# A layer kernel whose streamed operands lose the four padding columns between prompt and sample, and whose product halves meet at a bank border

## The chip, the core and the metric

The kernel runs on one core of a Trainium2 chip. A core has TensorE (PE: matmuls and their weight loads), VectorE (DVE), ScalarE (ACT), GpSimd (POOL) and SyncE (SP), which here issues loads; on-chip memory (SBUF) with 128 partitions, and PSUM, eight banks of 512 fp32 columns a partition, into which TensorE writes. The metric is the device time of one execution in microseconds.

## The reference

One layer of a streaming encoder, for 512 prompt frames of one new stream and 32 sample frames of a running one, width 1024:

```python
xn = rms_norm(x, g_mix_norm)
z = xn @ w_in
c_q, c_kv, k_r, u, gate_a, gate_b = jnp.split(z, IN_SPLITS, axis=-1)
...
attn = chunk_causal_mla(q_nope, q_rope, k_nope, kr_all, v, q_pos, jnp.arange(n_k))
u_c, lru_buf_new = causal_dwconv(u, lru_buf, lru_conv_w, lru_conv_b)
rec, h_last = rg_lru(u_c, h0, w_rg, b_rg, w_ig, b_ig, lru_lambda)
mixed = jax.nn.sigmoid(gate_a) * attn + jax.nn.sigmoid(gate_b) * rec
x = x + mixed @ w_out
up = rms_norm(x, g_ffn_norm) @ w_up
up_c, ffn_buf_new = causal_dwconv(up, ffn_buf, ffn_conv_w, ffn_conv_b)
gate, val = jnp.split(up_c, 2, axis=-1)
x = x + (jax.nn.silu(gate) * val) @ w_down
```

The convolutions have width 4 (u) and 3 (up), and start from stored rows of the sample's stream, or from zeros for the prompt; the recurrence starts from a stored state for the sample and from zero for the prompt.

## The kernel before

Channels lie on the 128 partitions and frames along a row. All frames are handled together: columns 0 to 511 are the prompt, then come four padding columns (`PAD`), then the 32 sample columns, so a row has `T` = 548 columns and a half `HT` = 274. The padding is there for the convolutions and the recurrence, which run once over the whole row: the last padding columns take the stored rows of the sample (L735 for U, L1555 for the up-projection), and the column before the sample restarts the recurrence (L587, L589).

The large products (`product`, L1612; `gate_half`, L1758; `output_product`, L1841; `last_product`, L2045) are fp32 products in three parts: the weight is split in a high part `w_hi` (ScalarE, L668) and a low part `w_lo` (VectorE, L1101), the operand likewise (`xnh`/`xnl`, `mxh`/`mxl`, `x2h`/`x2l`, `hh`/`hl`, type fp32r), and high x high, high x low and low x high are added up in PSUM. An item is 128 output channels: for each of 8 blocks k of 128 input channels (22 in the down-projection) three parts, and for each part two matmuls, one per half of the row, in two neighbouring banks. So an item of 8 blocks is 48 matmuls of 274 columns, each with its own weight load.

The order of the work:

1. Load and transpose x, its splits, and the products for the latents (L1651), which are 416 columns wide.
2. Twelve items of the first products (`FIRST`): gates A0, B0, U0 to U7, A1, B1, two bank pairs in turn (`pair`). VectorE evacuates each with `evacuate_first` (L1434) times the inverse norms `rsT`; for a U item the convolution (L1202, L1203, VectorE), the recurrence gates (`lru`, L1680, fp32 with the convolved `uc` as operand), activations on ScalarE (L745, L748, L755, L764, L771, L797) and the recurrence (L1214) follow. GpSimd keeps the tail of each U row (`conv_tail`, L582).
3. Eight head pairs of attention (`attend`), between which twelve more gate items are computed half by half (`gate_half`), and in which VectorE multiplies recurrence and gate (`gated_recurrence`, L1343) and ScalarE and VectorE evacuate keys, queries and values (L819, L850, L1283).
4. Eight items of the output product, the second norm, then 44 items of the up-projection (a loop of four with four bank pairs, `up_pair`). VectorE evacuates each (L1549), splits the weights two items ahead, sets two stored columns (L1555) and convolves (L1560 to L1565); for every second gate and value row ScalarE takes the SiLU (L1056) and GpSimd multiplies, rounds and subtracts (L630, L632, L634) to `hh` and `hl`. VectorE waits for these before it reuses the rows (L1561).
5. Eight items of the down-projection, 132 matmuls each; evacuation with the residual (L1585, L1582), transposes and stores.

Matmul j of a pair writes columns 0 to 273 of bank `2 * rank + j`, and an evacuation reads two runs of 274:

```python
PS[:, 2 * rank + j, 0:HT]
return PS[:, 2 * (g % 2):2 * (g % 2) + 2, 0:HT]
tt(halves(u_r[:, LEAD:]), up_pair(r), halves(rsT[:, :]), ALU.mult).then_inc(s_free, 1)
```

Of the kernel before, what the change touches and what calls it, by code (L numbers as in the profile page):

```python
# [15 lines left out]
F32 = mybir.dt.float32  # L16
# [4 lines left out]
P = 128  # L21
# [112 lines left out]
def layer(nc, i, c, o):  # L134
# [3 lines left out]
    with ctx:  # L138
# [33 lines left out]
        U = fixed("U", [P, KD, LEAD + T])  # L172
# [6 lines left out]
        QT = fixed("QT", [P, 4, T])  # L179
        xs = place  # L180
# [26 lines left out]
        TB = -(-T * 4 // 32) * 32  # L207
# [5 lines left out]
        ucs = [at(f"uc{s}", [P, T], uc_at[s]) for s in range(6)]  # L213
        a2 = at("a2", [P, 4, T], qt_at)
        ths = [a2[:, 3, :] if th_at[s] is None else at(f"th{s}", [P, T], th_at[s]) for s in range(6)]
        lruw = at("lruw", [P, 4, 2, P], v_at)
        tmps = [at("tmp0", [P, T], v_at + 4 * 2 * P * 4), at("tmp1", [P, T], p_at + 3 * TB)]

        assert region + D * 4 + 4 * P * 4 + NTT * P * 4 <= region + KD * (LEAD + T) * 4
# [22 lines left out]
        upx = fixed("upx", [P, 4, LEAD + T])  # L242
        uct = fixed("uct", [P, 4, T])
# [255 lines left out]
        def _(pool):  # L499
# [157 lines left out]
        def _(act):  # L657
# [71 lines left out]
            def first_tap(g, n):  # L729
# [5 lines left out]
                link(nc.scalar.activation(u_n[:, LEAD + S0 - 3:LEAD + S0], vec[:, V_CS:V_CS + 24].rearrange("p (j m) -> p m j", j=3)[:, n, :],  # L735
# [1390 lines left out]
```

## Time and profile before

| | |
|---|---|
| runs, us | 875.20, 871.04, 874.24 |
| median, us | 874.24 |
| span of the profiled execution, us | 872.8 |
| PE busy | 852.5 us, 98% |
| DVE busy | 568.6 us, 65% |
| ACT busy | 365.7 us, 42% |
| POOL busy | 192.9 us, 22% |
| clock granted to TensorE, mean | 0.992 |
| HBM traffic over the span | 72 GB/s |

The span goes from the first to the last instruction of the profiled execution; no separate time of that execution is listed, and the span lies among the three runs' times. PE is the matmuls, PEld their weight loads, which lie beside them. The page also follows the chain that ended last back from the end, gives groups of instructions by line and shape with the idle time before them and what ended it, and the trace can be asked for the instructions in order of time. Matmul records overlap, so a mean duration is not the time that one takes in a stream. The chain's shares by engine are PE 88%, ACT 6%, DVE 3%, issue 2%.

### The profile page before, as it was taken

What the parts mean: (1) busy time and instruction counts of PE and PEld (TensorE: products, weight loads), DVE (VectorE), ACT (ScalarE), POOL (GpSimd) and SP (SyncE); (2) the same over time, 40 slices, a digit from 0 to 9 for tenths busy, and PEclk for the clock granted to TensorE, in tenths of its full rate; (3) what the DMA queues carried; (4) which work ended last, traced back from release to release, by engine and by line L of the source; (5) the groups of instructions that cost most, each with busy time, mean ns of one, the idle gap of its engine ahead of it and who ended that gap; (6) DMA issues with size and microseconds to landing.
All of it is one profiled execution on the core that took longest, in us unless ns stands there. A gap on an engine that the chain in (4) does not pass through costs nothing.

```text
span 872.8 us, 16689 instructions
## 1 busy us (share of the span) xinstructions
PE 852.5 (98%) x6522; PEld 817.2 (94%) x6522; DVE 568.6 (65%) x998; ACT 365.7 (42%) x608; POOL 192.9 (22%) x206
## 2 busy tenths in 40 slices
PE   5999999899999999999999999999999999999998
PEld 5999898789999899877999999999999999999998
DVE  5586678867675676887656888778777876222121
ACT  5534959655655466556245221222212221122121
POOL 4021123202021121121140333323333234010000
PEclk8999999899999999999999999999999999999999
DMA  8433311131120101100223233232322323233321
GB/s 245 116 90 95 89 49 38 40 80 38 28 54 24 53 25 29 50 1 26 73 75 95 75 94 96 72 96 74 94 81 87 94 68 93 82 105 99 104 56 39
DMA packets 114466, 63.73 MB, mean 73 GB/s; under 512 B 7660, under 2 KB 112878, under 8 KB 114412
## 3 DMA queue, kind: packets, MB, share of 16 engines
q1 hardware_dynamic: 112428, 59.25, 24.0%
q0 software_dynamic: 1936, 3.70, 1.7%
q8 instruction: 38, 0.62, 0.3%
q14 instruction: 16, 0.13, 0.1%
q10 hardware_dynamic: 48, 0.02, 0.0%
HBM read 59.85 MB, written 2.70 MB: 72 GB/s over the span
## 4 chain that ended last, share of the span: by engine, by line
PE 88%; ACT 6%; DVE 3%; issue 2%; DMA 0%; POOL 0%; SPq 0%; ACTq 0%; DVEq 0%; POOLq 0%
PE PS L1612 49%; PE PS L1758 9%; PE PS L1841 6%; PE PS L1775 4%; PE PS L1813 4%; PE PS L1651 3%; PE PS L1717 2%; PE PS L1795 2%; PE PS L2045 2%; PE PS L1713 2%; PE PS L1749 2%; PE PS L1739 1%; PE PS L1680 1%; PE PS L1624 1%; PE PS L1820 1%
## 5 line engine op out<-in xcount | busy, mean ns | idle before, releaser
L668 ACT ACTIVATE w_hi<-w_raw 128x1024 fp32r<-128x1024 f32 (+2 forms) x102 | 105.5, 1035 | 316.5 <-PE PS L1612 301.4
L1101 DVE TENSOR_TENSOR w_lo<-w_raw,w_hi 128x1024 fp32r<-128x1024 f32 (+2 forms) x102 | 124.8, 1224 | 114.5 <-ACT w_hi L668 114.3
L1612 PE MATMUL PS<-x2h,w_hi 128*128 128x274 f32 x704 | 147.6, 291 | 0.0
L1612 PE MATMUL PS<-x2h,w_lo 128*128 128x274 f32 x704 | 147.0, 290 | 0.0
L1612 PE MATMUL PS<-x2l,w_hi 128*128 128x274 f32 x704 | 146.9, 290 | 0.0
L1612 PEld LDWEIGHTS PS<-x2l,w_hi 128*128 128x128 f32 x704 | 112.0, 189 | 0.0
L1612 PEld LDWEIGHTS PS<-x2h,w_hi 128*128 128x128 f32 x704 | 111.9, 189 | 0.1
L1612 PEld LDWEIGHTS PS<-x2h,w_lo 128*128 128x128 f32 x704 | 111.4, 189 | 0.0
L630 POOL TENSOR_TENSOR uct<-uct 128x548 f32<-128x548 f32 x22 | 30.2, 1373 | 176.4 <-DVE uct L1565 176.4
L1612 PE MATMUL PS<-hh,w_hi 128*128 128x274 f32 x308 | 64.7, 291 | 0.0
L1612 PE MATMUL PS<-hh,w_lo 128*128 128x274 f32 x308 | 64.6, 291 | 0.0
L1612 PE MATMUL PS<-hl,w_hi 128*128 128x274 f32 x308 | 64.2, 290 | 0.0
L1758 PE MATMUL PS<-xnh,w_hi 128*128 128x274 f32 x192 | 57.6, 300 | 0.2 <-DVE KT L1283 0.2
L1758 PE MATMUL PS<-xnl,w_hi 128*128 128x274 f32 x192 | 55.6, 290 | 0.0
L1758 PE MATMUL PS<-xnh,w_lo 128*128 128x274 f32 x192 | 55.6, 289 | 0.0
L887 ACT ACTIVATE PT<-PS 128x128 f32<-128x128 f32 (+4 forms) x72 | 31.3, 435 | 53.1 <-PE PS L1795 49.3
L1775 PE MATMUL PS<-KT,QT 100*128 100x128 f32 (+3 forms) x128 | 47.8, 456 | 3.5 <-ACT Pn L873 1.7
L562 POOL TENSOR_TENSOR rot<-Qn,rope 128x320 f32<-128x320 f32 x16 | 14.9, 948 | 162.7 <-DVE Qn L1273 162.7
L1612 PEld LDWEIGHTS PS<-hh,w_hi 128*128 128x128 f32 x308 | 48.9, 189 | 0.1
L1612 PEld LDWEIGHTS PS<-hl,w_hi 128*128 128x128 f32 x308 | 48.9, 190 | 0.0
L1612 PEld LDWEIGHTS PS<-hh,w_lo 128*128 128x128 f32 x308 | 48.8, 189 | 0.0
L1813 PE MATMUL PS<-PT,V 128*128 128x128 f32 x320 | 47.0, 278 | 0.0
(291 smaller groups left out, 1851.2 us busy)
## 6 DMA issues: line engine op xcount, KB each, us to landing
w_raw<-in_w_up_dram SPq DMA_DIRECT2D x44, 512.0 KB, 3.9
w_raw<-in_w_in_dram SPq DMA_DIRECT2D x24, 512.0 KB, 3.9
w_raw<-in_w_down_dram SPq DMA_DIRECT2D x16, 512.0 KB, 4.3
w_raw<-in_w_out_dram SPq DMA_DIRECT2D x8, 512.0 KB, 4.3
w_raw<-in_w_down_dram SPq DMA_DIRECT2D x8, 384.0 KB, 4.0
xnat<-in_x_prompt_dram SPq DMA_DIRECT2D x4, 512.0 KB, 5.4
w_raw<-in_w_in_dram SPq DMA_DIRECT2D x4, 416.0 KB, 7.4
wq<-in_w_q_b_dram SPq DMA_DIRECT2D x8, 192.0 KB, 2.5
```

The lines of the kernel that those rows point to most:

```text
L630: nc.gpsimd.tensor_tensor(uct[:, 2 + j, :], uct[:, j, :], uct[:, 2 + j, :], ALU.mult).then_inc(s_h2, 1)
L668: nc.scalar.activation(hi[:, slot % 2, 0:n], raw[:, slot % 4, 0:n], ACT.Copy).then_inc(s_hi, 1)
L887: nc.scalar.activation(PT[:, b, 0:w], PS[:, 6 + b, 0:w], ACT.Copy).then_inc(s_ptf, 1)
L1101: tt(lo[:, slot % 2, 0:n], raw[:, slot % 4, 0:n], hi[:, slot % 2, 0:n].bitcast(F32), ALU.subtract).then_inc(s_lo, 1)
L1612: last = mm(PS[:, 2 * rank + j, 0:HT], w[:, slot % 2, cols], x[:, k0 + k, j * HT:(j + 1) * HT], start=(k0 + k == 0 and first), stop=(k0 + ...
L1651: last = mm(PS[:, 3 + t, 0:LAT], x[:, k, w0:w0 + P], w[:, t4 % 2, cols], start=(k == 0 and w is hi and x is xnh), stop=(k == KD - 1 and w ...
L1713: last = mm(bank[:, a * P:(a + 1) * P], latT[:, k0:k0 + P], wkv[:, q % 2, 0, :], start=True, stop=True)
L1717: last = mm(bank[:, a * 2 * QK:(a + 1) * 2 * QK], cqT[:, k, c0 - p0:c0 - p0 + P], wq[:, q % 2, k, :], start=(k == 0), stop=(k == NQ - 1))
L1758: last = mm(PS[:, j, 0:HT], w[:, item % 2, cols], x[:, k, j * HT:(j + 1) * HT], start=(k == 0 and first), stop=(k == KD - 1 and w is lo))
L1775: mm(bank[:, 0:w], QT[0:QK + NT, 2 * par + h, t * P:(t + 1) * P], KT[0:QK + NT, 2 * par + h, 0:w], start=True, stop=True).then_inc(s_s, 1)
L1813: last = mm(values_bank(h)[:, t * P:(t + 1) * P], V[:, par, a, h:h + 2, :].rearrange("p h n -> p (h n)"), PT[:, b, a * P:(a + 1) * P], sta ...
L1841: last = mm(PS[:, 2 * (r % 4) + j, 0:HT], w[:, cols], x[:, k, j * HT:(j + 1) * HT], start=(k == 0 and first), stop=(k == KD - 1 and w is w ...
```

## The change

`T` becomes 544 and `HT` 272: xT, rsT, the split operands (`xnh`, `mxh`, `x2h`, `hh` and their low parts), the gates, the query columns and the sums have the sample right behind the prompt. The buffers on which a convolution or the recurrence runs (U, uc, th, a2, tmp, upx, uct) keep the padding: they have `TU` = 548 columns, and the fp32 products on `uc` halves of `HU` = 274. Where data go from one form to the other, the operation is split in a prompt part (512 columns) and a sample part (32): the evacuation of U and of the up-projection (`evacuate_padded`, 8 and 44 times), the product of recurrence and gate (8 times, written back without padding), and GpSimd's product of SiLU and value (22 times). Gate items and the others are evacuated in one operation.

In PSUM, the first half of a `product` is written to the last 272 columns of its bank and the second to the first 272 of the next one (`joined_half`), so that both are one run of 544 columns (`joined`), which an evacuation reads as such. `gate_half`, `output_product` and `last_product` write to the start of their banks as before.

The memsets of the padding of xT, cqT, rsT and sums go; two for U and upx come. All matmuls stay, 4704 of them with 272 columns in place of 274. As the rows are shorter, buffers move: the starts of w_hi, w_lo and of all split operands in SBUF were odd multiples of 32 bytes (but hl) and are multiples of 64 now.

```diff
-PAD = 4
-S0 = SEQ + PAD
+S0 = SEQ
 T = S0 + DEC
 HT = T // 2
+PAD = 4
 LEAD = 4
+US = SEQ + PAD
+TU = US + DEC
+HU = TU // 2
...
-        U = fixed("U", [P, KD, LEAD + T])
+        U = fixed("U", [P, KD, LEAD + TU])
...
+        place = max(place, qt_at + 4 * TU * 4)
...
-        upx = fixed("upx", [P, 4, LEAD + T])
-        uct = fixed("uct", [P, 4, T])
+        upx = fixed("upx", [P, 4, LEAD + TU])
+        uct = fixed("uct", [P, 4, TU])
...
+        def joined(bank):
+
+            return PS[:, bank:bank + 2, :].rearrange("p a b -> p (a b)")[:, 512 - HT:512 + HT]
+
+        def joined_half(bank, j):
+
+            return PS[:, bank + j, 0:HT] if j else PS[:, bank, 512 - HT:512]
+
         def pair(g):
 
-            return PS[:, 2 * (g % 2):2 * (g % 2) + 2, 0:HT]
+            return joined(2 * (g % 2))
...
-                    nc.gpsimd.tensor_tensor(uct[:, 2 + j, :], uct[:, j, :], uct[:, 2 + j, :], ALU.mult).then_inc(s_h2, 1)
+                    h_j = uct[:, 2 + j, 0:T]
+                    nc.gpsimd.tensor_tensor(h_j[:, 0:SEQ], uct[:, j, 0:SEQ], h_j[:, 0:SEQ], ALU.mult)
+                    nc.gpsimd.tensor_tensor(h_j[:, S0:], uct[:, j, US:], uct[:, 2 + j, US:], ALU.mult).then_inc(s_h2, 1)
                     pool.wait_ge(s_h2, it * 2 + (j + 1))
-                    nc.gpsimd.tensor_copy(one(hh, it * 2 + j, slice(None))[:, 0], uct[:, 2 + j, :]).then_inc(s_hh, 1)
+                    nc.gpsimd.tensor_copy(one(hh, it * 2 + j, slice(None))[:, 0], h_j).then_inc(s_hh, 1)
                     pool.wait_ge(s_hh, it * 2 + (j + 1))
-                    nc.gpsimd.tensor_tensor(one(hl, it * 2 + j, slice(None))[:, 0], uct[:, 2 + j, :],
+                    nc.gpsimd.tensor_tensor(one(hl, it * 2 + j, slice(None))[:, 0], h_j,
                                             one(hh, it * 2 + j, slice(None))[:, 0].bitcast(F32), ALU.subtract).then_inc(s_hl, 1)
...
-                nc.scalar.activation(uc(n), u_n[:, 1:1 + T], ACT.Identity, scale=vec[:, V_CW + n:V_CW + n + 1],
+                nc.scalar.activation(uc(n), u_n[:, 1:1 + TU], ACT.Identity, scale=vec[:, V_CW + n:V_CW + n + 1],
...
-            nc.vector.memset(xT[:, :, SEQ:S0], 0.0)
-            nc.vector.memset(cqT[:, :, SEQ:S0], 0.0)
             nc.vector.memset(ones[:, :], 1.0)
             nc.vector.memset(zero[:, :], 0.0)
-            nc.vector.memset(rsT[:, SEQ:S0], 1.0)
-            nc.vector.memset(sums[:, SEQ:S0], 1.0)
...
+            nc.vector.memset(U[:, :, LEAD + SEQ:LEAD + US], 0.0)
...
-                h_p = U[:, p, LEAD:]
+                h_p, g_p = U[:, p, LEAD:], gate("B", p)
                 dve.wait_ge(s_ends, 1)
                 dve.wait_ge(s_gt, gate_count("B", p))
-                stt(h_p, gate("B", p), 1.0, h_p, ALU.add, ALU.mult).then_inc(s_hb, 1)
+                stt(h_p[:, 0:SEQ], g_p[:, 0:SEQ], 1.0, h_p[:, 0:SEQ], ALU.add, ALU.mult)
+                stt(h_p[:, S0:T], g_p[:, S0:], 1.0, h_p[:, US:], ALU.add, ALU.mult).then_inc(s_hb, 1)
...
+            def evacuate_padded(dst, bank):
+
+                tt(dst[:, 0:SEQ], joined(bank)[:, 0:SEQ], rsT[:, 0:SEQ], ALU.mult)
+                tt(dst[:, US:TU], joined(bank)[:, S0:], rsT[:, S0:], ALU.mult).then_inc(s_free, 1)
+
             def evacuate_first(g):
 
                 kind, n = FIRST[g]
                 dve.wait_ge(s_used, I_IN + g + 1)
-                dst = U[:, n, LEAD:] if kind == "U" else gate(kind, n)
-                tt(halves(dst), pair(g), halves(rsT[:, :]), ALU.mult).then_inc(s_free, 1)
+                if kind == "U":
+                    evacuate_padded(U[:, n, LEAD:], 2 * (g % 2))
+                else:
+                    tt(gate(kind, n), pair(g), rsT[:, :], ALU.mult).then_inc(s_free, 1)
...
+            nc.vector.memset(upx[:, :, LEAD + SEQ:LEAD + US], 0.0)
...
-                    tt(halves(u_r[:, LEAD:]), up_pair(r), halves(rsT[:, :]), ALU.mult).then_inc(s_free, 1)
+                    evacuate_padded(u_r[:, LEAD:], 2 * r)
...
-                tt(halves(yT[:, m % 2, :]), pair(m), halves(xT[:, m, :]), ALU.add).then_inc(s_free, 1)
+                tt(yT[:, m % 2, :], pair(m), xT[:, m, :], ALU.add).then_inc(s_free, 1)
...
-                                last = mm(PS[:, 2 * rank + j, 0:HT], w[:, slot % 2, cols], x[:, k0 + k, j * HT:(j + 1) * HT],
+                                last = mm(joined_half(2 * rank, j), w[:, slot % 2, cols], x[:, k0 + k, j * HT:(j + 1) * HT],
...
-                        last = mm(PS[:, 4 + 2 * a + j, 0:HT], lruw[:, n % 4, a, :], uc(n)[:, j * HT:(j + 1) * HT], start=True, stop=True)
+                        last = mm(PS[:, 4 + 2 * a + j, 0:HU], lruw[:, n % 4, a, :], uc(n)[:, j * HU:(j + 1) * HU], start=True, stop=True)
```

VectorE's program in the up-projection, one item (the third) (st_127 is the buffer of kept tails). Before:

```order
L1549 TENSOR_TENSOR upx<-PS,rsT 128x548
L1101 TENSOR_TENSOR w_lo<-w_raw,w_hi 128x1024
L1555 COPY upx<-vec 128x2
L1561 TENSOR_SCALAR uct<-upx,vec 128x548
L1562 SCALAR_TENSOR_TENSOR uct<-upx,vec,uct 128x548
L1564 COPY st_127<-upx 128x4
L1565 SCALAR_TENSOR_TENSOR uct<-upx,vec,uct 128x548
```

And with the change, where L1443 and L1444 are `evacuate_padded`:

```order
L1443 TENSOR_TENSOR upx<-PS,rsT 128x512
L1444 TENSOR_TENSOR upx<-PS,rsT 128x32
L1115 TENSOR_TENSOR w_lo<-w_raw,w_hi 128x1024
L1575 COPY upx<-vec 128x2
L1581 TENSOR_SCALAR uct<-upx,vec 128x548
L1582 SCALAR_TENSOR_TENSOR uct<-upx,vec,uct 128x548
L1584 COPY st_127<-upx 128x4
L1585 SCALAR_TENSOR_TENSOR uct<-upx,vec,uct 128x548
```

The evacuation has become two instructions, and the second carries the signal that the banks are free; the rest is in the order it had. On TensorE no instruction changes its place.

## Rows read from the trace of the kernel before

**Rows 1.** The page: busy time, share of the span and instructions, all engines.

```profile
PE 852.5 (98%) x6522; PEld 817.2 (94%) x6522; DVE 568.6 (65%) x998; ACT 365.7 (42%) x608; POOL 192.9 (22%) x206
```

**Rows 2.** The chain that ended last, share of the span by line.

```profile
by line: PE PS L1612 49.4%; PE PS L1758 8.5%; PE PS L1841 5.7%; PE PS L1775 3.7%; PE PS L1813 3.5%; PE PS L1651 2.9%; PE PS L1717 2.0%; issue 2.0%; PE PS L1795 2.0%; PE PS L2045 1.9%; PE PS L1713 1.6%; PE PS L1749 1.6%; PE PS L1739 0.8%; PE
```

**Rows 3.** The same chain in order of time: start us, us, what.

```profile
85.93 0.74 DVE U L1434
...
114.70 0.74 DVE U L1434
...
228.56 1.11 PE PS L1749 x10
...
746.75 16.87 PE PS L1612 x132
```

**Rows 4.** TensorE by line and shape: xcount | busy us, mean ns | idle before.

```profile
L1612 PE MATMUL PS<-x2h,w_hi 128*128 128x274 f32 x704 | 147.6, 291 | 0.0
...
L1612 PE MATMUL PS<-hh,w_hi 128*128 128x274 f32 x308 | 64.7, 291 | 0.0
...
L1758 PE MATMUL PS<-xnh,w_hi 128*128 128x274 f32 x192 | 57.6, 300 | 0.2 <-DVE KT L1283 0.2
...
L1612 PE MATMUL PS<-xnh,w_hi 128*128 128x274 f32 x192 | 42.3, 302 | 0.0
...
L1841 PE MATMUL PS<-mxh,w_hi 128*128 128x274 f32 x96 | 20.7, 297 | 0.5 <-DVE mxl L1357 0.5
...
L2045 PE MATMUL PS<-hh,w_hi 128*128 128x274 f32 x44 | 10.3, 294 | 0.0
...
L1841 PE MATMUL PS<-mxh,out_hi 128*128 128x274 f32 x32 | 6.7, 291 | 0.0
```

**Rows 5.** TensorE in order of time, latent products: start us, us, engine, line.

```profile
25.16 0.35 PE L1651 MATMUL PS<-w_hi,xnh 128*128 128x416 f32 x1
...
32.71 0.35 PE L1651 MATMUL PS<-w_hi,xnl 128*128 128x416 f32 x1
```

**Rows 6.** VectorE in order of time, around 37 us and in the up-projection.

```profile
36.59 0.69 DVE L1153 COPY rsT<-PS 128x512 f32<-128x512 f32 x1 [4.12 <-PE PS L1663]
37.20 0.18 DVE L1154 COPY rsT<-PS 128x32 f32<-128x32 f32 x1
37.30 1.22 DVE L1101 TENSOR_TENSOR w_lo<-w_raw,w_hi 128x1024 fp32r<-128x1024 f32 x1
...
509.90 0.72 DVE L1549 TENSOR_TENSOR upx<-PS,rsT 128x548 f32<-128x548 f32 x1
```

**Rows 7.** Stretches: us, then busy us (xcount) of PE, PEld, DVE, ACT, POOL; granted clock.

```profile
170.00:377.00 207.00, 206.54 (x1639) 185.95 (x1640) 147.13 (x321) 114.71 (x232) 34.47 (x38) 1.00 0.15 40
...
377.00:386.00 9.00, 8.77 (x72) 7.00 (x70) 8.79 (x14) 5.86 (x12) 3.31 (x5) 1.00 0.01 2
...
464.00:746.00 282.00, 282.00 (x2207) 281.83 (x2205) 217.53 (x314) 68.63 (x74) 93.66 (x70) 1.00 0.29 85
...
153.80:160.60 6.80, 6.00 (x22) 4.70 (x21) 5.12 (x7) 4.73 (x10) 0.00 (x0) 0.50 0.36 93
```

**Rows 8.** GpSimd by line and shape.

```profile
L630 POOL TENSOR_TENSOR uct<-uct 128x548 f32<-128x548 f32 x22 | 30.2, 1373 | 176.4 <-DVE uct L1565 176.4
...
L529 POOL TENSOR_TENSOR krot<-nat,rope_in 128x80 f32<-128x80 f32 x4 | 1.3, 353 | 34.0 <-DVE nat L1194 34.0
```

**Rows 9.** TensorE in order of time, pairs of the first products.

```profile
60.10 0.41 PE L1612 MATMUL PS<-xnl,w_hi 128*128 128x274 f32 x2
60.35 0.42 PE L1612 MATMUL PS<-xnh,w_lo 128*128 128x274 f32 x2
60.62 0.41 PE L1612 MATMUL PS<-xnh,w_hi 128*128 128x274 f32 x2
```

**Rows 10.** Weight loads by line and shape.

```profile
L1612 PEld LDWEIGHTS PS<-x2h,w_hi 128*128 128x128 f32 x704 | 111.9, 189 | 0.1
...
L1749 PEld LDWEIGHTS PS<-wkv,latT 128*128 128x128 f32 x144 | 17.4, 191 | 1.9 <-ACT QT L921 1.2 <-ACT Qn L823 0.7
```

More of the change, by code:

```diff
@@ L204, in layer @@
         att_end = place
-        TB = -(-T * 4 // 32) * 32
+        TB = -(-TU * 4 // 32) * 32
         v1_at = v_at + NKT * 3 * VD * 4
@@ L212, in layer @@
         assert v1_at + 3 * TB <= p_at and p_at + 4 * TB <= att_end - NTT * 2 * HR * 4 and v_at + 4 * 2 * P * 4 + TB <= v1_at
-        ucs = [at(f"uc{s}", [P, T], uc_at[s]) for s in range(6)]
-        a2 = at("a2", [P, 4, T], qt_at)
-        ths = [a2[:, 3, :] if th_at[s] is None else at(f"th{s}", [P, T], th_at[s]) for s in range(6)]
+        ucs = [at(f"uc{s}", [P, TU], uc_at[s]) for s in range(6)]
+        a2 = at("a2", [P, 4, TU], qt_at)
+        ths = [a2[:, 3, :] if th_at[s] is None else at(f"th{s}", [P, TU], th_at[s]) for s in range(6)]
         lruw = at("lruw", [P, 4, 2, P], v_at)
-        tmps = [at("tmp0", [P, T], v_at + 4 * 2 * P * 4), at("tmp1", [P, T], p_at + 3 * TB)]
-        assert region + D * 4 + 4 * P * 4 + NTT * P * 4 <= region + KD * (LEAD + T) * 4
+        tmps = [at("tmp0", [P, TU], v_at + 4 * 2 * P * 4), at("tmp1", [P, TU], p_at + 3 * TB)]
+        assert region + D * 4 + 4 * P * 4 + NTT * P * 4 <= region + KD * (LEAD + TU) * 4
         xnat = at("xnat", [P, NTT, D], zone)
@@ L567, in mix @@
             def mix(p):
-                o_p, h_p = gate("A", p), U[:, p, LEAD:]
+                o_p, h_p = gate("A", p), U[:, p, LEAD:LEAD + T]
                 pool.wait_ge(s_o, 3 * p + 3)
@@ L580, in conv_tail @@
                 pool.wait_ge(s_free, n + 3)
-                tail = U[:, n, LEAD + T - 72:].rearrange("p (a b) -> p a b", b=36)[:, :, 33:36]
+                tail = U[:, n, LEAD + TU - 72:].rearrange("p (a b) -> p a b", b=36)[:, :, 33:36]
                 nc.gpsimd.tensor_copy(st[:, 2:8, n].rearrange("p (a b) -> p a b", a=2), tail).then_inc(s_tail, 1)
@@ L744, in lru_gates @@
                 act.wait_ge(s_tail, n + 1)
-                step.on(nc.scalar.activation(halves(u_n), PS[:, 4:6, 0:HT], ACT.Sigmoid, bias=vec[:, V_BR + n:V_BR + n + 1]))
+                step.on(nc.scalar.activation(halves(u_n), PS[:, 4:6, 0:HU], ACT.Sigmoid, bias=vec[:, V_BR + n:V_BR + n + 1]))
                 if n >= 2:
                     act.wait_ge(s_iu, n - 1)
-                nc.scalar.activation(halves(tmps[n % 2][:, :]), PS[:, 6:8, 0:HT], ACT.Sigmoid,
+                nc.scalar.activation(halves(tmps[n % 2][:, :]), PS[:, 6:8, 0:HU], ACT.Sigmoid,
                                      bias=vec[:, V_BI + n:V_BI + n + 1]).then_inc(s_lrui, 1)
@@ L789, in last_states @@
                 blocks = slice(0, KD)
-                ends = U[:, blocks, LEAD + T - 72:].rearrange("p n (a b) -> p n a b", b=36)[:, :, :, 35]
+                ends = U[:, blocks, LEAD + TU - 72:].rearrange("p n (a b) -> p n a b", b=36)[:, :, :, 35]
                 nc.scalar.activation(st[:, 0:2, blocks].rearrange("p a n -> p n a"), ends, ACT.Copy).then_inc(s_ends, 1)
@@ L1511, in _ @@
             dve.wait_ge(s_ri, NP_)
-            o_p, h_p = gate("A", 7), U[:, 7, LEAD:]
+            o_p, h_p = gate("A", 7), U[:, 7, LEAD:LEAD + T]
             dve.wait_ge(s_o, 3 * NP_)
@@ L1559, in up_block @@
                         dve.wait_ge(s_hl, it * 2 + 2)
-                    link(ts(dst, u_r[:, 2:2 + T], w[0], bias if is_value else None, ALU.mult, ALU.add) if is_value
-                         else ts(dst, u_r[:, 2:2 + T], w[0], None, ALU.mult))
-                    link(stt(dst, u_r[:, 3:3 + T], w[1], dst, ALU.mult, ALU.add))
-                    tail = u_r[:, LEAD + T - 72:].rearrange("p (a b) -> p a b", b=36)[:, :, 34:36]
+                    link(ts(dst, u_r[:, 2:2 + TU], w[0], bias if is_value else None, ALU.mult, ALU.add) if is_value
+                         else ts(dst, u_r[:, 2:2 + TU], w[0], None, ALU.mult))
+                    link(stt(dst, u_r[:, 3:3 + TU], w[1], dst, ALU.mult, ALU.add))
+                    tail = u_r[:, LEAD + TU - 72:].rearrange("p (a b) -> p a b", b=36)[:, :, 34:36]
                     step.on(nc.vector.tensor_copy(out_[:, bass.ds(it * 2 + (2 * b + m0), 1)][:, 0], tail))
-                    stt(dst, u_r[:, 4:4 + T], w[2], dst, ALU.mult, ALU.add).then_inc(s_gc, 1)
+                    stt(dst, u_r[:, 4:4 + TU], w[2], dst, ALU.mult, ALU.add).then_inc(s_gc, 1)
             up_block(0, 0)
```

16 lines of the change are left out of this document (8 added, 8 removed).

## Prediction

> **What bounds the kernel now.** I read the page's busy shares first. TensorE is busy for 852.5 of 872.8 us [rows 1], so an operation on another engine costs time only where it makes TensorE stop, and a column taken from a matmul is worth time only where TensorE itself is the chain. That is told by the chain that ended last, summed by line [rows 2]. The 274-column products make up L1612 49.4%, L1758 8.5%, L1841 5.7% and L2045 1.9% of the span, together 65.5% of 872.8 = 572 us. In order of time the same chain leaves TensorE in a few places only, among them from 85.93 us (the evacuation of U on VectorE, then ScalarE until 104.9) and from 114.70 us [rows 3]. The reader is to see that both begin with the very line that the change splits in two (L1434). Late in the program nothing leaves TensorE: 132 matmuls take 16.87 us as one piece [rows 3].
>
> How many matmuls there are: 704 + 308 + 192 + 192 + 96 + 32 + 44 = 1568 for the first of three operand pairs, and as many for each of the other two, so 4704 [rows 4]. What one costs can't be read from "mean 290 ns", since the records overlap; it is the distance from start to start. In a stream without a stop that is 16.87 us / 132 = 127.8 ns [rows 3]. So 572 us are about 4,470 matmuls on the chain; the other 230 stand beside ScalarE and VectorE work, and a column less in them is worth nothing.
>
> **The change, part by part.**
>
> *Two columns fewer in each of 4704 matmuls (274 to 272).* The trace has no 272, so the price of a column comes from two sizes of the same kind of product. The 416-column matmuls start at 25.16 and, 40 later, at 32.71 us: 188.8 ns each [rows 5]. The slope is (188.8 - 127.8)/(416 - 274) = 0.43 ns a column, and two are 0.86 ns. If the time were strictly in proportion, two columns would be 127.8 x 2/274 = 0.93 ns. I take 0.90, the middle. On the chain: 4,470 x 0.90 = 4.0 us gained. From below the price is bounded by nothing at all (rival B), from above by 1.7 ns (rival A).
>
> [...]
>
> *Evacuations of U and of the up-projection in two pieces* (8 and 44 times, L1434 and L1549). A 548-column one is 0.72 us and a 512-column copy from PSUM 0.69 [rows 6]. The 32-column copy behind it starts at 37.20 and lets the next go at 37.30: 0.10 us [rows 6]. So a split evacuation costs 0.69 + 0.10 - 0.72 = 0.07 us more; the ends are 0 (the columns left out pay for it) and the full record of the small one, 0.18. Of the 44 in the up-projection none is on the path: there VectorE is busy 217.5 of 282 us while TensorE is busy for all 282 [rows 7]; 44 x 0.07 = 3 us, even 44 x 0.18 = 8 us, go into 64 us of idle time. An up-projection item is 48 matmuls, 6.13 us, and a product waits only for the one four items back and for weights split an item ahead. Were that cover gone, it would cost those 3 us. Of the 8 evacuations of U, the two at 85.93 and 114.70 lie on the chain [rows 3]: 2 x 0.07 = 0.15 us, at most 2 x 0.18 = 0.36. Behind them wait ScalarE's first tap, and GpSimd's copy of the tail.
>
> *gated_recurrence in two pieces* (8 times, attention stage). Both operands lie in SBUF, which no split row shows; the same two bounds, 0 to 0.18 us each. From 170 to 377 us VectorE is busy 147 of 207 us and the split is covered; from 377 to 386 it is busy 8.79 of 9.00 [rows 7], in the last head pairs, so I take 2 x 0.07 = 0.15 us on the path, and 8 x 0.18 = 1.4 as the end.
>
> *GpSimd's product in two pieces* (22 times). It now takes 1.37 us; a small GpSimd operation of 80 columns takes 0.35 [rows 8]. 512 columns in proportion are 1.28, so the pair is up to 0.26 us longer. Behind it wait its own cast and subtraction, and behind these VectorE's reuse of the tile (L1561), inside VectorE's idle time again: 0. If it showed it would be 22 x 0.26 = 5.7 us.
>
> *Everything else.* The memsets of padding that go (xT, cqT, rsT, sums) run before the first data have arrived, and the two that come are 32 and 16 elements: 0. Operations on xT, rsT, gates, hidden values are 4 columns shorter: a few ns each, beside TensorE, 0. The convolution and recurrence keep 548 columns, since their buffers keep the padding. The single contiguous evacuation across the bank border has as many elements as the old one in two runs: 0 taken; none is on the path outside the two places named.
>
> Sum: -4.0 + 0.15 + 0.15 = **-3.7 us**. The page gives a span of 872.8 us, which lies 1.4 below the median of the three runs (874.24) and inside their spread (871.04 to 875.20). 872.8 - 3.7 = 869.1 for a profiled span, and against the median 874.24 - 3.7 = **870.5 us**. A measurement can tell about 0.5% here, 4.4 us: the forecast is a real gain that lies just inside that bound.
>
> **The rivals.**
>
> *A, more than two columns' worth (chance 0.22).* A row was 2192 bytes and its second half began 1096 bytes in; now they are 2176 and 1088. If TensorE took the streamed operand in groups of four columns, 274 columns would touch 69 groups and 272 touch 68, both halves now starting on a group: 4 x 0.43 = 1.7 ns per matmul, 4,470 x 1.7 = 7.7 us, with the 0.3 of cost -7.4, hence 866.8. For it: two pairs of equal shape stand 0.25 and 0.27 us apart [rows 9], so something beside the count of columns sets the distance, and 127.8 ns is more than 274 columns at 2.4 GHz (114.2). Against it: the 416-column products, whose rows are whole groups, carry 188.8 - 173.3 = 15.5 ns above their columns, no less than the 13.6 of the 274.
> The Trainium skill, page "SBUF — State Buffer", section "Specifications (TRN2)", speaks of 16-byte cachelines, with a penalty at each cross to a new one; by that rule the estimate is this rival's.
>
> *B, the weight load is the bound (0.08).* Each matmul has its own load, with records of 189 ns that don't shrink. If the load set the distance, two columns would be worth 0 and only the 0.3 us of cost would be left: 874.5. Against it: ten 128-column fp32 matmuls take 1.11 us, 111 ns each [rows 3], with loads whose records are 191 ns, as long as those of the products [rows 10]. So a load can follow another within 111 ns, less than 127.8.
>
> *C, slower: the new starting places collide (0.06).* Both halves and the weights now all start at multiples of 64 bytes, and every first half is written at column 240 of its bank rather than 0. If the streamed reads then met the weight reads, every pair could cost what the slow pair does, 0.27 us or 135 ns per matmul [rows 9]: 135 - 0.9 - 127.8 = +6.3 ns, 4,470 x 6.3 = +28 us. It decides where the distance comes out above 127.8 + (4.4 - 0.3)/4,470 = 128.7 ns. I put a mild case of it, +2 ns, at 883. Against it: the early pairs on xnh [rows 9] and the late stream on hh [rows 3] start at different places and mix, and both come to 128 to 130 ns.
>
> *D, the clock (0.14).* From 153.80 to 160.60 us the granted clock is 0.50, that is 1.2 GHz, behind a stretch in which the chain ran over ScalarE and VectorE; for 6.0 of these 6.8 us TensorE was busy [rows 7]. A shifted schedule can lose such a dip or get another one; one is worth at most half of its 6.8 us, 3.4. So -3.7 becomes -7.1 (867.1) or -0.3 (873.9), with equal chances. The spread of the three runs before, 4.2 us, is of that size.
>
> **How the numbers follow.** The forecast has the remaining 0.50; its own spread (0.83 to 1.0 ns per matmul, cost 0 to 1.8 us) reaches from about -4.5 to -2, and a quarter of it lies beyond -4.4. Faster by over 0.5%: 0.50 x 0.25 + 0.22 + 0.07 = 0.42. Within 0.5%: 0.375 + 0.08 + 0.07 = 0.52. Slower by over 0.5%: 0.06. The range takes in A with a little more (865.0) and the side of B and D without the last tenths (874.2); C and the far ends are left out.
>
> **What would show it.** In the up-projection 48 matmuls of 272 columns should take 6.09 us where 6.13 stand now, a distance of 126.9 ns; 126.1 is A, 127.8 is B, above 128.7 is C. VectorE's busy time should rise by 4 to 10 us, GpSimd's by up to 6, and TensorE should still never wait in the up-projection. The granted clock row by stretches tells D. The forecast is wrong if the distance falls by more than 1.2 or less than 0.6 ns, or if TensorE's idle time grows by over 1 us.

## The result and the profile after

| | before | after |
|---|---|---|
| median of the runs, us | 874.24 | 863.08 |
| lowest and highest | 871.04 to 875.26 | 861.39 to 864.23 |
| span of the profiled execution | 872.8 | 860.8 |
| mean granted clock | 0.992 | 0.994 |

The ratio is 0.9879, with a 95% interval of 0.9863 to 0.9894: faster by 1.2%, below the whole range of the forecast (865.0 to 874.2). The medians lie 11.2 us apart, where the forecast had 3.7. The profiled execution of the change took 863.08 us.

The page's busy times of the changed kernel, to be laid beside [rows 1]:

```profile
PE 840.1 (98%) x6522; PEld 804.8 (93%) x6522; DVE 572.7 (67%) x1056; ACT 365.6 (42%) x608; POOL 199.2 (23%) x228
```

TensorE is busy for 12.4 us less, about as much as the span is shorter (12.0); nothing that the change did to waits is needed to explain it. The chain that ended last, in order of time (start us, us, what), beside [rows 3]:

```profile
40.65 6.01 PE PS L1632 x48
...
83.66 0.69 DVE U L1443
84.35 0.11 DVE U L1444
...
112.34 0.69 DVE U L1443
113.03 0.11 DVE U L1444
...
461.03 275.87 PE PS L1632 x2202
737.12 16.54 PE PS L1632 x132
```

The same pieces of the kernel before, three more rows of its chain:

```profile
42.31 6.11 PE PS L1612 x48
...
465.18 281.35 PE PS L1612 x2202
```

The reader is to see three things. 132 matmuls take 16.54 us where [rows 3] have 16.87: 125.3 ns instead of 127.8, a fall of 2.5 ns for two columns. From the start of the up-projection to the end of the span it is 860.8 - 461.03 = 399.77 us against 872.8 - 465.18 = 407.62; the 7.85 us are 2.51 ns for each of the 2202 + 7 x 132 = 3126 matmuls there. And the rest: 2.5 us between the first product and the up-projection (420.38 against 422.87), and 1.66 us before 40.65, where no product of the change has run yet. This last part is no gain of the change: in the profiles of the experiments below the first product starts anywhere from 40.5 to 43.2 us, with the columns of before as well as with the new ones. The stretches (us, busy us of PE, PEld, DVE, ACT, POOL, clock), beside [rows 7]:

```profile
149.00:162.00 13.00, 10.70 (x51) 8.69 (x52) 9.78 (x21) 10.74 (x22) 0.00 (x0) 0.74 0.27 65
170.00:377.00 207.00, 206.64 (x1651) 185.92 (x1650) 148.11 (x331) 115.92 (x235) 33.63 (x37) 1.00 0.15 40
461.00:737.00 276.00, 276.00 (x2206) 276.00 (x2205) 221.08 (x358) 68.87 (x75) 100.13 (x92) 1.00 0.30 87
```

TensorE never stops in the up-projection (276.00 of 276.00), though VectorE has 221 us of work there in a shorter time. The clock falls around 154 us as before (0.74 over these 13 us in both profiles). GpSimd by line and shape, beside [rows 8]:

```profile
L643 POOL TENSOR_TENSOR uct<-uct 128x512 f32<-128x512 f32 x22 | 28.4, 1292 | 165.1 <-DVE uct L1585 165.1
...
L644 POOL TENSOR_TENSOR uct<-uct 128x32 f32<-128x32 f32 x22 | 12.5, 567 | 0.0
```

### The profile page after: what moved, and what is told of

Same layout as the page of the kernel before. It is cut to its first block, busy times and chain, and to the rows that moved or that the text cites. A ratio compares the mean times of both kernels' runs of the same rounds, so it can differ in the third digit from the quotient of the medians.

```text
span 860.8 us, 16769 instructions
## 1 busy us (share of the span) xinstructions
PE 840.1 (98%) x6522; PEld 804.8 (93%) x6522; DVE 572.7 (67%) x1056; ACT 365.6 (42%) x608; POOL 199.2 (23%) x228
## 4 chain that ended last, share of the span: by engine, by line
PE 88%; ACT 6%; DVE 3%; issue 2%; DMA 1%; SPq 0%; ACTq 0%; DVEq 0%
PE PS L1632 49%; PE PS L1778 9%; PE PS L1861 6%; PE PS L1795 4%; PE PS L1833 4%; PE PS L1671 3%; PE PS L1737 2%; PE PS L1815 2%; PE PS L2065 2%; PE PS L1733 2%; PE PS L1769 2%; DMA xnat<-in_x_prompt_dram 1%; PE PS L1759 1%; PE PS L1700 1%; PE PS L1840 1%
## 5 line engine op out<-in xcount | busy, mean ns | idle before, releaser
L1115 DVE TENSOR_TENSOR w_lo<-w_raw,w_hi 128x1024 fp32r<-128x1024 f32 (+2 forms) x102 | 127.3, 1249 | 104.8 <-ACT w_hi L682 104.8
L1632 PE MATMUL PS<-x2h,w_hi 128*128 128x272 f32 x704 | 145.7, 288 | 0.0
L1632 PE MATMUL PS<-x2h,w_lo 128*128 128x272 f32 x704 | 145.7, 288 | 0.0
L1632 PE MATMUL PS<-x2l,w_hi 128*128 128x272 f32 x704 | 145.1, 288 | 0.0
L643 POOL TENSOR_TENSOR uct<-uct 128x512 f32<-128x512 f32 x22 | 28.4, 1292 | 165.1 <-DVE uct L1585 165.1
L1632 PE MATMUL PS<-hh,w_hi 128*128 128x272 f32 x308 | 64.2, 289 | 0.0
L1632 PE MATMUL PS<-hh,w_lo 128*128 128x272 f32 x308 | 63.7, 288 | 0.0
L1632 PE MATMUL PS<-hl,w_hi 128*128 128x272 f32 x308 | 63.5, 288 | 0.0
L1778 PE MATMUL PS<-xnh,w_hi 128*128 128x272 f32 x192 | 57.2, 298 | 0.2 <-DVE KT L1294 0.2
L1778 PE MATMUL PS<-xnh,w_lo 128*128 128x272 f32 x192 | 55.6, 290 | 0.0
L1778 PE MATMUL PS<-xnl,w_hi 128*128 128x272 f32 x192 | 55.1, 287 | 0.0
```

Of the source, the lines that this page charges most:

```text
L643: nc.gpsimd.tensor_tensor(h_j[:, 0:SEQ], uct[:, j, 0:SEQ], h_j[:, 0:SEQ], ALU.mult)
L1115: tt(lo[:, slot % 2, 0:n], raw[:, slot % 4, 0:n], hi[:, slot % 2, 0:n].bitcast(F32), ALU.subtract).then_inc(s_lo, 1)
L1632: last = mm(joined_half(2 * rank, j), w[:, slot % 2, cols], x[:, k0 + k, j * HT:(j + 1) * HT], start=(k0 + k == 0 and first), stop=(k0 + k ...
L1778: last = mm(PS[:, j, 0:HT], w[:, item % 2, cols], x[:, k, j * HT:(j + 1) * HT], start=(k == 0 and first), stop=(k == KD - 1 and w is lo))
```

## The experiments

The question was where 1.6 ns of the 2.5 come from, if a column is worth 0.43 ns. The distance below is always the time from the start of one matmul to the start of the next, in the mean of a block. My theory: the count of 274 and the second half's start at column 274, 8 bytes past a multiple of 16, each cost by themselves. Rivals: a column is worth more than the slope; the place in PSUM; where the buffers lie; the length of the rows; the joined evacuation.

In the sweeps the down-projection's blocks 1 to 6 each get their own form of the matmul (block 0 and the last one stay), so one profile compares six. In these blocks columns are left out or read twice, or other columns or weights are read, so that the rows of y that they make are not the layer's. A block's row in the chain divided by 132 is the distance.

**1. Where the streamed operand starts.** 264 columns, read s columns late:

```diff
-last = mm(joined_half(2 * rank, j), ..., x[:, k0 + k, j * HT:(j + 1) * HT],
+last = mm(joined_half(2 * rank, j)[:, 0:264], ..., x[:, k0 + k, j * HT + s:j * HT + s + 264],
```

> Blocks 1 to 6 of the down-projection of the changed kernel run with 264 columns in each half, read from columns 0, 1, 2, 4, 8 and 3 after the start of the half (other data are multiplied, y is wrong there), written to the same place in PSUM. If the start of the streamed operand is the cause: start 0 is fastest, starts 4 and 8 (still a multiple of 16 bytes) within 0.3 ns of it, starts 1, 2, 3 (4, 8, 12 bytes past one) 2 to 3 ns slower. If not: all six within 0.5 ns of each other.

The chain of this kernel in order of time, s = 0, 1, 2, 4, 8, 3:

```profile
736.99 15.99 PE PS L1637 x132
...
753.53 16.39 PE PS L1637 x132
...
770.47 16.35 PE PS L1637 x132
...
787.36 15.96 PE PS L1637 x132
...
803.87 16.20 PE PS L1637 x132
...
820.62 15.93 PE PS L1637 x132
```

In ns: 121.1, 124.2, 123.9, 120.9, 122.7, 120.7. With the same count of columns the start alone is worth up to 3.5 ns. But it is no plain rule of 16 bytes, and two of the six came out otherwise than expected: s = 3 is as cheap as 0 and 4, and s = 8 costs 1.6.

**2. Where the result goes in PSUM.** 264 columns to column v of the bank, v = 0, 2, 4, 8, 248, 16:

```diff
-last = mm(joined_half(2 * rank, j), ...
+last = mm(PS[:, 2 * rank + j, v:v + 264], ...
```

> Blocks 1 to 6 of the down-projection of the changed kernel run with 264 columns in each half, both halves written from column 0, 2, 4, 8, 248 and 16 of their banks (the evacuation reads other columns in part, y is wrong there). If the place in PSUM (the bank border) is worth something, 0 and 248 differ by 1 ns or more; if it is the streamed operand alone, all six are within 0.5 ns.

```profile
739.11 15.99 PE PS L1637 x132
...
805.26 15.99 PE PS L1637 x132
```

Each of the six rows reads 15.99 or 16.00 us (the two shown are v = 0 and v = 248), so the place in the bank is worth nothing.

**3. The kernel before with all its 548 columns, split 272 + 276** (the halves also meet at a bank border):

```diff
-last = mm(PS[:, 2 * rank + j, 0:HT], ..., x[:, k0 + k, j * HT:(j + 1) * HT],
+last = mm(joined_half(2 * rank, j), ..., x[:, k0 + k, HS[j]],
+HS = [slice(0, 272), slice(272, 548)]
```

> The kernel before with its 548 columns, split 272 + 276 instead of 274 + 274, halves meeting at the bank border in all pairs of products. Columns in all are as before. Start theory: the second half now starts a multiple of 16 bytes into the row, so most of the gain comes without a column less: the up-projection's 48 matmuls from 6.13 to about 6.05 to 6.08 us, the time 866 to 870. Count theory (one matmul of 272, one of 276, 0.43 ns a column): 6.13, the time as before (874). Group-of-four theory: 274 costs 276, so the pair falls from 276 + 276 to 272 + 276, 0.85 ns per matmul, 870.

867.91 us (863.15 to 868.79), ratio 0.9925 (0.9897 to 0.9954). A block of its down-projection:

```profile
740.55 16.68 PE PS L1623 x132
```

126.4 ns, 1.4 less than before, and not one column has gone. The count theory expected nothing, and the groups of four 0.85 ns. From the up-projection on it takes 403.14 us, 4.5 less than before.

**4. The count of columns.** Both halves of N columns, starts at 0 and 272, N = 270, 268, 264, 256, 262, 266:

```diff
-last = mm(joined_half(2 * rank, j), ..., x[:, k0 + k, j * HT:(j + 1) * HT],
+last = mm(joined_half(2 * rank, j)[:, 0:N], ..., x[:, k0 + k, j * HT:j * HT + N],
```

> In the down-projection of the changed kernel, blocks 1 to 6 run their 132 matmuls with 270, 268, 264, 256, 262 and 266 columns in each half instead of 272, from the same starts (the last columns of each half are left out, so y is not complete there). The starts stay at multiples of 64 bytes. If count and meeting of reads both work by what the starts give, the distances lie on a line from 125.25 ns at 272 down to 121.1 at 264 (0.5 ns a column): 270 124.2, 268 123.2, 266 122.2, 262 120.1, 256 117. If operands go in groups of four columns, 270 stands with 272 and 266 with 268; in groups of sixteen, 256 alone is lower.

```profile
737.97 16.60 PE PS L1637 x132
...
755.12 16.37 PE PS L1637 x132
...
772.03 16.00 PE PS L1637 x132
...
788.58 15.63 PE PS L1637 x132
...
804.76 16.33 PE PS L1637 x132
...
821.63 16.25 PE PS L1637 x132
```

In ns: 125.8, 124.0, 121.2, 118.4, 123.7, 123.1. From 256 to 272 the slope is (125.3 - 118.4)/16 = 0.43 ns, what the prediction had. But the counts between lie neither on the line that I had expected nor in steps of four: 262 columns take 2.5 ns longer than 264, and 270 take 0.5 longer than 272. Odd counts were not measured.

**5. Both reads of the pair.** 264 columns, (shift of the streamed operand, shift of the weights) = (0, 8), (8, 8), (1, 1), (0, 1), (0, 4), (0, 16):

```diff
+ws = shift of the weights, but 0 for the last k
-last = mm(..., w[:, slot % 2, k * P:(k + 1) * P], ...
+last = mm(..., w[:, slot % 2, k * P + ws:(k + 1) * P + ws], ...
```

> Down-projection of the changed kernel, 264 columns in each half, blocks 1 to 6 with the streamed operand read x columns later and the weights of all but every eighth k loaded from w columns later (other data are multiplied, y is wrong there): (x, w) = (0, 8), (8, 8), (1, 1), (0, 1), (0, 4), (0, 16). Known: (0, 0) 121.1, (8, 0) 122.7, (1, 0) 124.2 ns. If the two reads meet, only the difference of their places counts: (8, 8) and (1, 1) come back to 121.1 within 0.5 ns, and (0, 8) and (0, 1) are slower. If it is the streamed operand's own start: (8, 8) 122.7, (1, 1) 124.2 and all with x = 0 at 121.1. If it is the weights' own start: (0, 1) is slow too, and (1, 1) slowest.

The first two of the six, (0, 8) and (8, 8):

```profile
736.40 16.19 PE PS L1638 x132
...
753.13 16.02 PE PS L1638 x132
```

Measured 122.7, 121.4, 124.0, 122.2, 122.3, 121.9 ns, where (0, 0) has 121.1, (8, 0) 122.7 and (1, 0) 124.2. Shifting both by 8 takes back nearly all that a shift of one costs: where the two reads stand to each other counts. Shifting both by 1 takes nothing back (124.0). So at least two effects lie in a start; which mechanisms they are isn't shown.

**6 and 7. Where the buffers lie, and the length of a row.** The changed kernel with every buffer 32 bytes higher, and with 548 columns from row to row of which 544 are used:

```diff
-        base = 16512
+        base = 16544
```

```diff
-        xnh = fixed("xnh", [P, KD, T], F32R)
+        xnh = fixed("xnh", [P, KD, TU], F32R)[:, :, 0:T]
```

> The changed kernel with every buffer in SBUF moved up by 32 bytes, so that all operands start at odd multiples of 32 bytes again, as before, and their distances from each other stay. If what counts is the place relative to the weights, or the half's start within the row, the time stays at 863 and the distance at 125.3. If the multiple of 64 counts by itself, the distance goes up by 1 ns or more, 4 us or more in all.

> The changed kernel with 272-column halves, but the rows of the split operands 548 columns apart as before, so that a row starts at a multiple of 16 bytes only and the halves 1088 bytes apart. If the 272 columns and the half's start at a multiple of 16 bytes are the whole gain, 863 and 125.3 ns. If the row's stride of a multiple of 64 bytes bears part, the distance lies between 125.3 and 126.9 and the time between 863 and 869.

862.63 us (859.04 to 864.55), ratio 0.987 (0.9835 to 0.9905); and 864.14 (863.26 to 864.69), 0.9895 (0.9873 to 0.9917). Their blocks take 16.54 and 16.50 us. Neither the multiples of 64 bytes nor the row length is the cause; with the longer rows the up-projection's piece takes 276.40 us for 275.87, 0.2 ns a matmul.

**8. Count and start apart, in the kernel before.** (Start of the second half, columns of each) = (272, 274), (274, 272), (272, 272), (272, 276), (276, 272), (276, 268):

```diff
-last = mm(..., x[:, k0 + k, j * HT:(j + 1) * HT],
+last = mm(..., x[:, k0 + k, j * v[0]:j * v[0] + v[1]],
```

> The kernel before, whose output blocks 1 to 6 of the down-projections (start of the second half in a row of 548, columns in a matmul of either half) have (272, 274), (274, 272), (272, 272), (272, 276), (276, 272), (276, 268) columns; halves overlap or leave columns out, so y is wrong there. Block 0 stays as before, halves of 274 from columns 0 and 274: 127.7 ns between starts. Theory 'the count': 272 columns give 125.2 from whichever column the second half starts, 274 columns 127.3 to 127.7, 276 about 127. Theory 'the start': the second half at 274 lies 8 bytes past a multiple of 16, and half of the matmuls pay for it: (274, 272) then gives 126 or more against 125.2 of (272, 272), and (272, 274) 126 to 126.5. Both together, as I hold it: (272,272) 125.2, (272,276) 126.0 to 127.0, (272,274) 126.5 to 127.5, (274,272) 126 to 127, (276,268) about 124 to 125.

```profile
744.73 16.78 PE PS L1617 x132
...
762.05 16.66 PE PS L1617 x132
...
779.26 16.52 PE PS L1617 x132
...
796.33 16.93 PE PS L1617 x132
...
813.80 16.51 PE PS L1617 x132
...
830.86 16.30 PE PS L1617 x132
```

In ns 127.1, 126.2, 125.2, 128.3, 125.1, 123.5, beside 127.8 for (274, 274) [rows 3]. Moving only the start gives 0.7, cutting only the count 1.6, both 2.6. At 0.43 ns a column 0.9 of the 1.6 are the two columns, so 0.7 belong to the count of 274 itself, 0.7 to the start at 274, and 0.3 show only when both go. The third form is the change's, on the longer rows of before, and has the change's distance. Both halves of my theory hold, with two misses: (272, 276) came out above the range that I had given (128.3), (276, 268) below it (123.5). Moving the start also moves the streamed operand against the weights, and this run doesn't part the two.

**9. Unequal halves of 544 columns**, first half of 264, 256, 248, 280, 240, 288:

```diff
-last = mm(joined_half(2 * rank, j), ..., x[:, k0 + k, j * HT:(j + 1) * HT],
+last = mm(PS[:, 2 * rank + j, 0:(T - v if j else v)], ..., x[:, k0 + k, (v if j else 0):(T if j else v)],
```

> The changed kernel with rows of 544 columns, in the down-projections split unequally: first half of 264, 256, 248, 280, 240, 288 columns for blocks 1 to 6, the rest in the second. Block 0 stays 272 + 272 at 125.3 ns. If only the count of columns in steps of 8 matters, on a line, every split gives the same 125.3 within 0.4. The sweep of one count for both halves put 264 at 121.1, which is 0.6 under the line from 256 (118.4) to 272 (125.3): if that is so because of the count alone and 280 lies on the line (128.7), 264 + 280 gives 124.9. If the place at which the second half starts matters by more than 16 bytes, the splits differ by more than that.

The last of the six, 288 + 256:

```profile
824.35 16.39 PE PS L1637 x132
```

In the mean of both halves 125.5, 124.8, 125.2, 126.7, 125.6 and 124.2 ns. The hope for 264 + 280 failed (125.5, 126.7 the other way round), but 288 + 256 is 1.1 ns under 272 + 272.

**10 and 11. The bank border alone.** The changed kernel with both halves at the start of their banks and evacuations in two and three pieces; and the kernel before, 274 + 274 with its padding, but with halves that meet:

```diff
-                tt(dst[:, 0:SEQ], joined(bank)[:, 0:SEQ], rsT[:, 0:SEQ], ALU.mult)
-                tt(dst[:, US:TU], joined(bank)[:, S0:], rsT[:, S0:], ALU.mult).then_inc(s_free, 1)
+                tt(dst[:, 0:HT], PS[:, bank, 0:HT], rsT[:, 0:HT], ALU.mult)
+                tt(dst[:, HT:SEQ], PS[:, bank + 1, 0:SEQ - HT], rsT[:, HT:SEQ], ALU.mult)
+                tt(dst[:, US:TU], PS[:, bank + 1, SEQ - HT:HT], rsT[:, S0:], ALU.mult).then_inc(s_free, 1)
```

```diff
-                tt(halves(dst), pair(g), halves(rsT[:, :]), ALU.mult).then_inc(s_free, 1)
+                tt(dst, pair(g), rsT[:, :], ALU.mult).then_inc(s_free, 1)
```

> The changed kernel, 272 columns each half without padding, but both halves at the start of their banks again, and evacuated as before in two runs with a gap, so without the meeting at the border. If the whole gain is in the matmul's distance: 863 +- 1 us, ratio to before 0.986 to 0.989, VectorE's busy time as in the changed kernel or a few us over it, matmul distances the same 125.3. If the joined evacuation is worth something on the path, up to 1.5 us more: 864 to 865.

> The kernel before with its 274 + 274 columns and padding, but with a product's halves meeting at the bank border. If the place in PSUM is worth nothing, as its sweep showed: ratio to before 0.998 to 1.002, distances 127.6 to 127.8. If the join is part of the gain: 0.997 or less.

864.80 us (863.77 to 866.47), ratio 0.9901 (0.9878 to 0.9924); and 873.59 (870.71 to 874.74), ratio 1.000 (0.9985 to 1.0015). The border brings the kernel before nothing. In the changed one the time alone can't tell: 864.80 lies where I had expected it if the join were worth something, 1.7 us over the median with it, and the two intervals overlap. So the two chains are compared; this is the one without the join:

```profile
42.26 6.00 PE PS L1633 x48
...
462.75 275.86 PE PS L1633 x2202
738.83 16.54 PE PS L1633 x132
```

From its first product to its up-projection 420.49 us (the change: 420.38), from there to the end of the span 862.5 - 462.75 = 399.75 (399.77). Nearly the whole difference of the two profiles stands before the first product, 42.26 against 40.65. So the meeting at the border is worth nothing measurable. The profile of the kernel before with joined halves has its first product at 40.56 and its up-projection at 461.09, and its clock of 0.998 shows no fall around 154 us:

```profile
149.00:162.00 13.00, 10.37 (x65) 8.41 (x64) 11.69 (x29) 12.16 (x24) 0.00 (x0) 1.00 0.27 65
```

Its span is 868.7 us, 4.1 less than the kernel before in its own profile, at the same distances and a ratio of 1.000: so much one execution differs from another through the start (1.75 us) and that dip (2.3 us between the first product and the up-projection).

**12. Larger counts, both starts on large multiples.** N = 288, 284, 280, 276, 274, 272, halves from columns 0 and 256:

```diff
-last = mm(joined_half(2 * rank, j), ..., x[:, k0 + k, j * HT:(j + 1) * HT],
+last = mm(PS[:, 2 * rank + j, 0:N], ..., x[:, k0 + k, 256 * j:256 * j + N],
```

> The changed kernel; in the down-projections of blocks 1 to 6 both halves have 288, 284, 280, 276, 274 and 272 columns, from columns 0 and 256 of the streamed row, which overlap, so y is wrong there; all starts are multiples of 1,024 bytes from the row's own. Block 0 is 272 + 272 at 125.3 ns. With the half_sweep's 128.2 for 276 and 127.1 for 274, and the split's 130.6 for 288, the theory 'a count that is no multiple of 8 pays by itself' expects 272: 125.2, 274: 127, 276: 128, 280: about 128.5, 284: 131 to 132, 288: 130.6. Then 284 is slower than 288. The theory 'only the start of the second half matters' expects a straight line of 0.43 ns a column: 126.1 for 274, 126.9 for 276, 128.7 for 280, 130.4 for 284, 132.1 for 288.

```profile
738.38 17.52 PE PS L1637 x132
...
756.45 17.39 PE PS L1637 x132
...
774.38 16.87 PE PS L1637 x132
...
791.79 16.72 PE PS L1637 x132
...
809.06 16.85 PE PS L1637 x132
...
826.45 16.57 PE PS L1637 x132
```

In ns 132.7, 131.7, 127.8, 126.7, 127.7, 125.5. 274 columns cost 2.1 ns more than 272, though every start is a large multiple, and 1.0 more than 276: the count pays by itself. The straight line fails, and so does my rule of multiples of 8: 284 came out at 131.7 as expected, but 288 at 132.7 and not at 130.6, and 276 is, for its size, cheap here (126.7 for 128) and was dear in 8 (128.3), where the second half started at 272. A count's price hangs together with the starts.

**13. The changed kernel split 288 + 256 in every product.**

```diff
+HA = 288
+HS = [slice(0, HA), slice(HA, T)]
-last = mm(..., x[:, k0 + k, j * HT:(j + 1) * HT],
+last = mm(..., x[:, k0 + k, HS[j]],
```

> The changed kernel with its 544 columns split 288 + 256 in every product instead of 272 + 272; the halves meet at a bank border as before. The split sweep gave 124.1 ns in the mean of the two for it against 125.3. If that holds in the whole kernel it is 1.1 to 1.2 ns on each of some 4,470 matmuls of the path, 5 us: about 858 us, ratio to before 0.981 to 0.984. If the longer first half makes the evacuations or anything else late, or the sweep's gain was special to the down-projections, 860 to 863.

858.94 us (858.22 to 859.39), ratio to before 0.9828 (0.9807 to 0.9849), the fastest kernel of this study; its interval lies wholly below the one of the change.

```profile
734.08 16.37 PE PS L1635 x132
```

124.0 ns. From the up-projection on 856.7 - 461.05 = 395.65 us, 4.1 less than the change.

**14. The change's columns without its halves**: 544 columns, split 274 + 270 by the same edit.

> The changed kernel, its padding gone and 544 columns in every product, but split 274 + 270, so that the first half keeps the 274 columns of before and the second starts at column 274, 8 bytes past a multiple of 16. The same number of columns leaves the matmuls as in the change. If fewer columns alone were worth what came out, the mean distance is 125.3 and the time 863. If, as I now hold, the columns are worth 0.9 ns and the rest is what a count of 274 (or 270) and such a start cost, the mean distance is 126.5 to 127.3 and the time 868 to 871, ratio to before 0.993 to 0.997.

868.71 us (864.10 to 868.95), ratio 0.9928 (0.9904 to 0.9953).

```profile
741.73 16.73 PE PS L1635 x132
```

126.7 ns. As many columns leave as in the change, and 403.50 us from the up-projection on are 4.1 us less than before, not 7.85. In 3 the form of the halves changed and no column went (4.5 us), here the columns go and the halves keep a start at 274 (4.1 us); the change does both and gets 7.85. The two don't add up exactly, since 276 and 270 have prices of their own:

| columns, split | from the up-projection to the end, us | less than before |
|---|---|---|
| 548, 274 + 274 | 407.62 | |
| 548, 274 + 274, joined | 407.61 | 0.0 |
| 548, 272 + 276 | 403.14 | 4.5 |
| 544, 274 + 270 | 403.50 | 4.1 |
| 544, 272 + 272 (the change) | 399.77 | 7.85 |
| 544, 288 + 256 | 395.65 | 12.0 |

## Why the prediction was wrong

**The bound held.** TensorE was the bound in the late stages, nothing stops it in the up-projection (busy for 276.00 of 276.00 us), and the matmuls carry the gain.

**The step that failed is "two columns fewer", 0.90 ns per matmul.** It was mis-sized: 2.51 ns in the 3126 late matmuls, and in the earlier ones on the path 2.5 us in all. For all matmuls the forecast had 4.0 us of gain, 3.7 with the small costs; measured are 7.85 + 2.49 = 10.3 us, these costs already taken off. The slope itself was right: 0.43 ns a column again, from 256 to 272. What was wrong is that I put 274 on that line. It lies above it, by the count and by the start of the second half (8 and 12), and the change left both behind together with the columns. Taking the same columns away with a count of 274 and a start at 274 gives 4.1 us in the late stages, 1.3 ns each (14), still over the 0.90. The 0.83 ns at the low end of the forecast's own spread is in no run as the price of two columns; the slope gives 0.86, the change gave 2.51. A slip in the chances beside it: a spread that ends at -4.5 can't have a quarter of itself beyond -4.4.

**The sign was in the trace before.** From start to start, the down-projection of the kernel before has 126.0 ns behind a first half and 129.5 behind a second (means over about 65 each): equal counts, but the half that starts at column 274 takes longer. After the change it is 125.6 and 124.9. I saw that pairs differ [rows 9], and took it for something that sets a level, not for a part of what the edit removes. And my argument against rival A compared with the 416-column products, which are another product; against the 272-column ones of the change the 274 carry 13.6 - (125.3 - 113.3) = 1.6 ns more above their columns at 2.4 GHz. That is the missing part.

**Rival A** had the direction, that more than two columns' worth goes, and gave 1.7 ns; it was too small and its rule is not the right one. Groups of four columns would make 262 and 264 alike (66 groups from either start), and they differ by 2.5 ns (4); a start at column 3 touches one group more than at 0 and costs nothing (1). This was rival A's form of the rule that the Trainium skill, "SBUF — State Buffer", section "Specifications (TRN2)", gives for 16-byte cachelines: such a penalty may be part of the start's price, but these rows (2.5 ns between 262 and 264, 0.4 ns less at column 3 than at 0) don't follow it alone.

**Rival B** is refuted: the distance moved with every size, down to 118.4 ns at 256 columns, with the same loads.

**Rival C** is refuted for this kernel (125.3, not over 128.7), and neither the column in the bank (2) nor the multiple of 64 bytes (6) matters. Its thought, that streamed reads and weight reads get in each other's way, has something to it: a relative shift of 8 columns costs 1.6 ns and a common one gives 1.3 of it back, though a common shift of 1 column gives nothing back (5).

**Rival D.** The dip near 154 us stayed. At the start the clock row gives 0.91 over the first 20 us where 0.85 stood, part of the 1.66 us there. The joined kernel before has the same 0.91 there, so it is no effect of the change. In that kernel the dip near 154 us was absent, and the stretch from the first product to the up-projection took 420.53 us for 422.87: the dip is worth about 2.3 us, inside the 3.4 that the prediction allowed. Since the dip is in both profiles of the main comparison, it doesn't make the difference between them.

**The small costs.** A split evacuation of U on the chain is 0.69 + 0.11 us for 0.74: +0.06, forecast 0.07. VectorE's busy time rose by 4.1 us (forecast 4 to 10). GpSimd's pair is in the mean 1.29 + 0.57 = 1.86 for 1.37 us, +0.49 and not +0.26, but this mean hides two kinds. 15 of the 22 small pieces take 0.25 to 0.27 us, less than the 0.35 that I had taken. The other seven take 1.23 to 1.24; each began while VectorE was at its split of the weights (`w_lo`, L1115) and ended 0.11 us behind it:

```profile
523.35 1.83 DVE L1115 TENSOR_TENSOR w_lo<-w_raw,w_hi 128x1024 fp32r<-128x1024 f32 x1
524.06 1.23 POOL L644 TENSOR_TENSOR uct<-uct 128x32 f32<-128x32 f32 x1
```

So the term that the sum left out is this meeting, and not the piece's own size. Its cover held as forecast: GpSimd's busy time rose by 6.3 us (up to 6 forecast) and TensorE still never waited. The gated recurrence's 0.15 us and the border's 0 can't be told from nothing in the rows (420.38 and 420.49 us).

**What stays open.** Why the distance isn't a smooth function of the count, why 276 costs 128.3 ns with one start of the second half and 126.7 with another, and why 288 + 256 is cheaper than 272 + 272. The runs show that the count, the start and the place relative to the weights matter; no mechanism was shown. In the earlier stages the gain per matmul was not taken apart. Its sum of 2.5 us repeats: among the profiles with the same 0.74 around 154 us, the sweep on the kernel before (8) has 422.71 us from the first product to the up-projection, and those on the changed kernel (1, 2, 4) 420.24 to 420.43.

## What to carry to other kernels

Where matmuls of a fixed size set the end, the number and place of the streamed columns is worth a sweep by itself: a split of the same columns can bring as much as taking columns away. Before pricing "n columns fewer" by a slope, look at the distance behind each form of matmul apart, and ask what else the edit changes in it, the count itself and the column at which the second half starts. Give each block of a long uniform stage its own form, and one profile compares six.

## What was not expected of the hardware

- 262 fp32r columns take 123.7 ns and 264 take 121.2; 274 take 127.7 and 276 take 126.7: fewer columns can be slower.
- At 264 columns a streamed operand that starts 4 bytes later costs 3.1 ns more per matmul, 12 bytes later nothing (120.7 ns for 121.1); moving the weights alone by 1 to 16 columns costs 0.8 to 1.6.
- 544 columns split 288 + 256 take 124.0 ns in the mean, split 272 + 272 they take 125.3.
- The column in the PSUM bank doesn't show in the distance (15.99 to 16.00 us for 132 matmuls at six starts).
- A 32-column product on GpSimd takes 245 to 266 ns in 15 of 22 cases and 1230 to 1243 ns in the seven that ran beside VectorE's weight split, nearly as long as a 512-column one (1292): a mean of 567 ns fits neither.
